# Turned units of a two-block transformer kernel: the 512-column products of both column blocks ahead of the 256-column ones

## The reference, cut to what matters

```python
qkv = jnp.einsum('bsd,de->bse', h, w_qkv[l])                      # 2048 x 6144, then three kinds of attention
x = x + jnp.einsum('bse,ed->bsd', y, w_o[l])
h = rmsnorm(x, ffn_norm[l])
g = causal_dwconv(jnp.einsum('bsd,df->bsf', h, w_gate[l]), conv_w[l], conv_b[l])    # 2048 x 5632
u = jnp.einsum('bsd,df->bsf', h, w_up[l])
x = x + jnp.einsum('bsf,fd->bsd', jax.nn.silu(g) * u, w_down[l])
...
x = x + jnp.square(jax.nn.relu(hm @ w_up[l])) @ w_down[l]         # second block, 2048 x 8192 and back
```

## Time and profile before

| | us |
|---|---|
| median of three runs | 2459.22 |
| lowest, highest | 2454.11, 2463.85 |
| the profiled execution | 2454.48 |
| its span, first to last instruction | 2452.7 |
| PE busy | 2403.1 |
| weight loads on PE | 2012.3 |
| DVE busy | 1562.8 |
| ACT busy | 1248.1 |

### The profile page before, as it was taken

How to read it: one execution, slowest core, us unless ns; L and a number is a source line. 1 busy time by engine, 2 the same in 40 slices (tenths; PEclk the granted TensorE clock), 3 DMA queues, 4 the chain that set the end, 5 groups by cost and what they waited for, 6 DMA issues and landing times.

```text
span 2452.7 us, 32017 instructions
## 1 busy us (share of the span) xinstructions
PE 2403.1 (98%) x12314; PEld 2012.3 (82%) x12314; DVE 1562.8 (64%) x2437; ACT 1248.1 (51%) x1954; POOL 5.2 (0%) x12
## 2 busy tenths in 40 slices
PE   7999999999999999999999999999999999999998
PEld 6888877788888888888877877887888888888886
DVE  5687777777777557755667544664766556556454
ACT  5466566555555435544556445655544344344343
POOL 0000000000000000000000000000000000000000
PEclk9999999999999999999999999999999999999999
DMA  6544444455555565566564544554565665665664
GB/s 232 168 159 155 137 155 138 155 185 193 198 181 193 195 188 180 194 210 187 165 192 144 172 131 135 185 166 132 172 196 182 197 180 196 190 188 185 212 188 138
DMA packets 119063, 432.13 MB, mean 176 GB/s; under 512 B 13264, under 2 KB 13536, under 8 KB 118400
## 3 DMA queue, kind: packets, MB, share of 16 engines
q1 hardware_dynamic: 117936, 424.70, 54.3%
q0 software_dynamic: 976, 5.39, 0.6%
HBM read 427.93 MB, written 2.11 MB: 175 GB/s over the span
## 4 chain that ended last, share of the span: by engine, by line
PE 92%; DVE 4%; ACT 2%; issue 1%; DMA 1%; SPq 0%; ACTq 0%; DVEq 0%
PE bank L456 28%; PE bank L465 15%; PE bank L467 15%; PE bank L466 15%; PE bank L458 14%; DVE lo_w L1270 1%; PE bank L653 1%; DVE xT L1409 1%; ACT hi_w L840 1%; PE bank L482 1%; ACT xT L944 0%; DMA raw_w<-in_w_qk 0%; PE bank L637 0%; PE bank L526 0%; PE bank L607 0%
## 5 line engine op out<-in xcount | busy, mean ns | idle before, releaser
L1270 DVE TENSOR_TENSOR lo_w<-raw_w,hi_w 128x1024 fp32r<-128x1024 f32 x804 | 965.9, 1218 | 631.0 <-ACT hi_w L840 630.0
L840 ACT ACTIVATE hi_w<-raw_w 128x1024 fp32r<-128x1024 f32 x804 | 833.8, 1052 | 606.3 <-PE bank L467 417.8
L456 PE MATMUL bank<-xT,hi_w 128*128 128x512 f32 x3008 | 1054.0, 395 | 0.0
L458 PE MATMUL bank<-xT,lo_w 128*128 128x256 f32 x3008 | 839.5, 279 | 0.0
L456 PEld LDWEIGHTS bank<-xT,hi_w 128*128 128x128 f32 x3008 | 565.8, 188 | 128.8 <-issue 0.3
L458 PEld LDWEIGHTS bank<-xT,lo_w 128*128 128x128 f32 x3008 | 568.8, 189 | 0.5
L465 PE MATMUL bank<-hi_w,act_hi 128*128 128x512 f32 x864 | 341.4, 395 | 0.0
L467 PE MATMUL bank<-hi_w,act_lo 128*128 128x512 f32 x864 | 341.2, 395 | 0.0
L466 PE MATMUL bank<-lo_w,act_hi 128*128 128x512 f32 x864 | 341.2, 395 | 0.0
L465 PE MATMUL bank<-hi_w,xT 128*128 128x512 f32 (+1 forms) x736 | 294.2, 400 | 4.3 <-DVE xT L1409 3.5
L467 PE MATMUL bank<-hi_w,xT 128*128 128x512 f32 (+1 forms) x736 | 286.7, 389 | 0.0
(11 more groups left out here) (315 smaller groups left out, 1586.5 us busy)
## 6 DMA issues: line engine op xcount, KB each, us to landing
raw_w<-in_w_up SPq DMA_DIRECT2D x216, 512.0 KB, 4.2
raw_w<-in_w_down SPq DMA_DIRECT2D x216, 512.0 KB, 3.6
raw_w<-in_w_gate SPq DMA_DIRECT2D x88, 512.0 KB, 3.7
raw_w<-in_w_in SPq DMA_DIRECT2D x72, 512.0 KB, 3.8
raw_w<-in_w_qk SPq DMA_DIRECT2D x64, 512.0 KB, 3.6
raw_w<-in_w_v SPq DMA_DIRECT2D x32, 512.0 KB, 4.0
raw_w<-in_w_o SPq DMA_DIRECT2D x32, 512.0 KB, 3.5
raw_w<-in_w_out SPq DMA_DIRECT2D x32, 512.0 KB, 3.6
```

Source lines behind the costliest of these rows:

```text
L456: e.matmul(pair[c][:, :], w_hi[:, cols_k], both[:, kt].rearrange("p h t -> p (h t)"), start=(kt == 0), stop=False, skip_group_check=True)
L458: last = e.matmul(pair[c][:, 0:TOK], w_lo[:, cols_k], both[:, kt, 0, :], start=False, stop=(kt == g.kts - 1), skip_group_check=True)
L840: e.activation(hi_w[:, u % SPLIT_SLOTS, 0:unit_cols[u]], raw_w[:, u % RAW_SLOTS, 0:unit_cols[u]], ACT.Copy).then_inc(s["w_hi"], 1)
L1270: e.tensor_tensor(lo, raw_w[:, u % RAW_SLOTS, 0:unit_cols[u]], hi.bitcast(F32), ALU.subtract).then_inc(s["w_lo"], 1)
```

## The change

Only the order of PE's products within a turned unit changes. Before, the unit's first column block is done for all its rows of tiles, then the second. Now, for each row of tiles, the two 512-column products (c=0, c=1) come first and the two 256-column ones (c=0, c=1) behind them. The number of products, their operands and their sizes stay. `w_used` still goes up twice in a unit, now with the last two products of it, where it was with the last of each half.

```diff
@@ -447,17 +447,24 @@
                         e.wait_ge(s[name], count)
                     if g.fresh:
                         input_landed(g, u)
+                    if g.kind == "turned":
+                        both = turned_in(g.stage)
+                        for k in range(g.per):
+                            kt = (u - g.first) * g.per + k
+                            half = [slice(k * TURNED_COLS + c * P, k * TURNED_COLS + (c + 1) * P) for c in range(2)]
+                            for c in range(2):
+                                e.matmul(pair[c][:, :], w_hi[:, half[c]], both[:, kt].rearrange("p h t -> p (h t)"),
+                                         start=(kt == 0), stop=False, skip_group_check=True)
+                            for c in range(2):
+                                last = e.matmul(pair[c][:, 0:TOK], w_lo[:, half[c]], both[:, kt, 0, :],
+                                                start=False, stop=(kt == g.kts - 1), skip_group_check=True)
+                                if k == g.per - 1:
+                                    last.then_inc(s["w_used"], 1)
+                        continue
                     for c in range(2):
                         for k in range(g.per):
                             kt = (u - g.first) * g.per + k
-                            if g.kind == "turned":
-                                both = turned_in(g.stage)
-                                cols_k = slice(k * TURNED_COLS + c * P, k * TURNED_COLS + (c + 1) * P)
-                                e.matmul(pair[c][:, :], w_hi[:, cols_k], both[:, kt].rearrange("p h t -> p (h t)"),
-                                         start=(kt == 0), stop=False, skip_group_check=True)
-                                last = e.matmul(pair[c][:, 0:TOK], w_lo[:, cols_k], both[:, kt, 0, :],
-                                                start=False, stop=(kt == g.kts - 1), skip_group_check=True)
-                            else:
+                            if g.kind == "straight":
                                 in_hi, in_lo = straight_in(g.stage)
                                 at = kt if g.stage.startswith("down") else 12 + kt if g.stage == "ox" else g.k0 + kt
                                 rows, cols_k = slice(c * P, (c + 1) * P), slice(k * g.width, (k + 1) * g.width)
```

## The result

| | before | after |
|---|---|---|
| median of 20 runs each, us | 2461.14 | 2465.18 |
| lowest, highest | 2453.54, 2466.32 | 2462.15, 2469.29 |
| the profiled execution | 2454.48 | 2462.80 |
| its span | 2452.7 | 2461.0 |

Two things in the table need an explanation beside the medians: the profiled executions are 8.3 us apart and the medians 4.0, and the runs of before scatter over 13 us, those of after over 7.

What follows compares the result with a forecast made beforehand. PE's stream of weight products was taken as the bound, busy for 98% of the span. Stream 0, gate-group waits 5.2 and other groups 1.4 us gave +6.6, on a median of 2459.22, so 2465.8 us; range 2451 to 2480.

Steps and rivals of the forecast that it cites:

- the likeliest case: Whole kernel: the forecast as summed, slower by 3 to 11 us, given 54%.
- The late release: Gate groups' ends: bank 0 evicted later, so PE waits 0.25 us for DVE's split at 21 of 22, 5.2 us.
- a shift of 0.78: Gate group's end: ACT and DVE's string of evictions and additions, and DVE's split behind it, move 0.78 us later, not 1.27.
- The first rival: Gate groups: the string moves by 1.27 us, PE waits 0.74 at 21 places, 17 us in all, 2476 us; 19%.
- extra lead: First gate group: DVE's split ready 0.5 us earlier before PE's load than in the other 21, so no wait counted.
- The sign announced: Profile after: a line of PE waiting for DVE's lo_w behind gate groups, some 21 entries and 5 us.
- The stream: PE's products in turned units: four products take 0.693 us in the new order as in the old, 0 us.
- The loads rival: PE's turned units: two 256-column products in a row are bound by their weight loads, up to +109 us, 2575 us; 5%.
- The other epilogues: Ends of the 28 qk, kx, qx, q_nope and k_nope groups: small delays, 1.4 us of at most 24; up groups free.
- The faster rival: PE's stream: half of what is paid above the columns is saved, 42 us, 2424 us; 8%.

Runs made afterwards that it cites:

- Experiment 1: Kernel before, only the w_used increment for column block 0 moved to the 512-column product ahead of the unit's last: 2464.36 us against 2459.07, ratio 1.0024.
- experiment 3: Changed kernel, but the last turned unit of each group keeps the order of before: 2459.98 us, ratio 1.0002 to before.
- experiment 4: Changed kernel's loop, column block by column block, 512, 512, 256, 256 within one bank, early release: 2460.07 us, ratio 1.0001 to before.
- experiment 5: Changed kernel, but ACT and DVE split the next unit's weights before a gate group's end: 2457.71 us against 2460.58 of before, ratio 0.9990.
- experiment 7: Kernel before profiled three more times: 2463.97, 2459.01, 2458.75 us; also before with the split ahead of the gate group's end: 2461.22 against 2462.83, ratio 1.0000.
- the twos: Orders with two 512-column products, then two of 256, as in the change (2465.18 us against 2461.14 of before); undisturbed units 2.7867 us.
- the split-ahead version: Kernel before, with ACT and DVE splitting the next unit's weights before a gate group's end: 2461.22 us against 2462.83, ratio 1.0000; profiled at 2463.99.
- Fours: Changed kernel's loop, per bank four 512-column products, then four of 256: one profiled execution, 2468.11 us, units 2.8067 us.
- eights: Changed kernel's loop, all eight 512-column products of a unit, then all eight of 256: one profiled execution, 2461.37 us, units 2.7933 us.

## Why the prediction was right, and where it wasn't

**The time** was forecast at 2465.8 and measured at 2465.18, in the range of 2451 to 2480; the likeliest case, slower by less than 0.5%, came in. That the two times are 0.6 us apart is luck. The difference was forecast at 6.6 and measured at 4.0 (4.7 by the ratio), on a median of before that was 1.9 us higher with 20 runs than with the three of the forecast; and within the difference a cost that was left out and one that was overlooked in before nearly cancel.

**The late release** was right in its mechanism, its place and nearly its size: a shift of 0.78 forecast, 0.79 read; a wait of 0.25 us forecast, 0.19 to 0.22 measured, since the dearer units that the forecast didn't have gave the split 0.04 us more; 5.2 us in all against 4.7. Experiment 1 shows it without the new order, experiments 3, 4 and 5 take it away in two ways (the early release, the split ahead). The first rival (the whole delay comes through) was wrong for 21 of the 22 groups, since DVE's split did cover the rest. It was right for the one group that the prediction had counted out for its 0.5 us of extra lead: there the shift was 1.61, the lead 1.23, and the wait 0.46, the longest of all. The sign announced, a line of waits with some 21 entries, didn't come in the change, since the record ahead leaves only 0.13 us of each gap; it came in experiment 1, with waits of 0.24 and more.

**The stream** is where a step failed: "Sum of the stream: 0.693 again, 0 us". It was composed from neighbours seen one at a time, 512 behind 512 in a straight unit and 256 ahead of 512 in a turned one, at 0.227 and 0.12. On average the steps came out as 0.233, 0.233, 0.115 and 0.116: the long ones dearer than forecast, the short ones cheaper, and 0.6967 in sum, that is 0.0033 more, 5.2 us over 390 units. The trace of before had a warning. Its straight units don't agree among themselves: 12 products of 512 columns take 2.720 us in the stage of the earlier trace rows (0.2267 each) and 2.800 us in the down stages (0.2333 each), so 512 behind 512 had no single price to take over. The difference is below what starts rounded to 0.01 us can show, and needed long stretches. The loads rival, with 4 ns a four as its bound, was nearer than its 5% said, though its mechanism (256 behind 256 waits for the load) didn't hold: those products are 0.115 apart, closer than 0.12.

**What cancelled it** was in the trace of before and not read. Twenty of its units run at 2.83; I took the rate of pairs from two stages that were in the faster rhythm and took it for the only one. Before's order is some 4.5 us slower in an execution like the three of experiment 7 than its fastest rhythm would be, and the twos aren't in any of their five profiles. Sum as the runs show it, against an execution of before with 85 slow units: 4.7 + 5.2 - 4.5 = 5.4 us, where the medians say 4.0 and the ratio 4.7; against the first profile: 4.7 + 5.2 - 1.1 = 8.8, where the spans say 8.3. The same sum for experiments 3, 4 and 5, which have no waits: 4 to 5 less 4.5, about 0, where 1.0002, 1.0001 and 0.9990 were measured. How many slow units the timed executions had is not on record, so that 85 is typical of them is argued from three profiles. Before's scatter of 12 us at one mean clock (experiment 7) is of the size that the second rhythm gives: its profiles had 20 to 88 slow units, the split-ahead version's 205, which is 1.1 to 10.9 us. The granted clock has its share in the rest.

**The other epilogues** were put at 1.4 us, "one twentieth" of 24, which would be 1.2. They were nothing: in up2, with its 32 groups, no unit of the changed kernel differs from its neighbours by more than a nanosecond but for those five, at the start of the stage or of a phase, that are longer before as well, and the first 128 units, with the 16 qk groups, end 0.1 us later than before.

**The faster rival** did not happen. The Trainium skill, page "TensorE: Matmul & The Clock Gate", section "Back-to-back issue gap", would have a pair at 0.325 us by its formula, which it gives for an isolated product. No order tried here came nearer than 0.3467, before's own. The measurement decides: for this type and with a new weight load for each product the figure wasn't reached by any of these orders.

**A metric that doesn't see it.** PE's busy share is 98% before and after, and the weight loads' is 82% both times, with 2012.3 and 2014.0 us. The Trainium skill, page "Perfetto Trace Analysis", section "Identifying the Most-Contended Engine", says that matmul busy time is not a good measure of how close a kernel is to its limit, which these rows bear out, and names the busy share of weight loads instead. Here that one doesn't see the loss either: records of 0.19 us overlap at steps of 0.12, their covered time stays where it is while the kernel loses 8 us, and 8 us are 0.3% of the span, too little for a share in whole per cent. (A busy time counts overlapping records once and isn't their sum: 3008 products of 395 ns would be 1188 us, and the earlier trace rows says 1054.0.)

**The best version of the change** is the one with the split ahead of the gate group's end, at 0.9990 of before (0.9978 to 1.0002): no longer slower, and not clearly faster.

**Left open.** What in PE sets the lengths, the steps of 6.67 ns, and which of the two rhythms a stretch falls into. Each stretch keeps its rhythm from one interruption of PE to the next (a wait, or straight units in between), and the split-ahead version of before, whose PE program is before's, had 125 slow units in gate and up1 where before had one. That the moment of the restart chooses is argued from that, not shown; no experiment set that moment on purpose. A stretch at 1.2 GHz near the start of a stage doesn't choose: experiment 1 had one at 1747 and ran up2 at 2.773, the split-ahead version of before had none there and ran it at 2.827 all the same.

## What to carry to other kernels

Moving a product moves its semaphore. Before an order of products is changed, follow the release to whatever stands behind the waiting engine in program order, and compare the shift with the lead of the next thing that the bounding engine needs; here 0.58 us of lead and 0.78 of shift made 21 waits of 0.2. Look at the first and last instance by themselves; the one with the most lead had the longest wait. If the lead is too short, put the urgent instruction ahead of the wait rather than the release back where it was.

Take the rate of a stream over tens of products, in every stage, and from more than one execution. A stream that looks periodic can have a second period 2% longer; the first profile of before was 6.7 us under the median, and between the profiles of one order the slow units made a difference of 3 to 10 us.

## What the runs showed of the hardware that wasn't expected

A stream of alternating 512- and 256-column fp32r products, each with its own weight load, at the full granted clock, runs at 0.3467 or at 0.3533 us a pair, and stays in either for as long as 125 units (some 350 us). Products in twos showed one rhythm only, 0.6967 us a four, in five profiles. Fours have 0.7017 and eights 0.6983 for the same work, each in one profile. Straight units of 512-column products run at 0.2267 us a product in some stages and at 0.2333 in others. At the granted clock of 1.2 GHz the same products take exactly their columns: pairs start at 470.19 and 472.11 us, three pairs apart, which is 0.64 us each, where the profile of before has a granted clock of 0.50. (The record of the clock starts at 15.4 us; for the earlier trace rows, at 13 us, the level is read from the same 0.64.)
